# Moving one VectorE subtraction ahead in the turnover between two sub-layers

## The chip, the cores and the metric

The program runs on one core of a Trainium2 chip: TensorE (PE; its weight loads are shown as PEld), VectorE (DVE), ScalarE (ACT), GpSimd (POOL) and SyncE (SP), which issues the weight transfers. The engines run their own instruction streams in order and meet only at semaphores. The metric is the device time of one execution in microseconds; lower is better.

## The reference, cut to what matters

Two groups of tokens, 128 context tokens and 256 latent ones (384 columns together), go through two layers. A layer is SwiGLU, token mixing, SwiGLU, so there are six sub-layers. Each is wrapped in the same way:

```
def pre_norm(x, mod, j, g):
    return rmsnorm(x, g) * (1 + mod_chunk(mod, 3 * j + 1)) + mod_chunk(mod, 3 * j)

def post_residual(x, out, mod, j, g, w):
    return x + w * mod_chunk(mod, 3 * j + 2) * rmsnorm(out, g)

xs = post_residual(xs, swiglu(pre_norm(xs, mod_s, 0, ...), w_in, w_out), mod_s, 0, norm_post, 0.5)
```

All is fp32. The change sits where `post_residual` of one sub-layer meets `pre_norm` of the next.

## The kernel before, in words

Activations lie with the model dimension on the partitions: X is eight tiles (d = 0 to 7) of 128 x 384. The input h of a sub-layer is also eight tiles, and each is kept as two numbers whose sum is the fp32 value: a high part HH, rounded by ScalarE to the type that TensorE multiplies in, and a low part HL, the rest. Weights are split likewise into WH and WL. A product is three matmuls: WH with HH, WH with HL, WL with HH.

Weights stream through a ring of six 1 MB slots (RAW); SyncE loads them, ScalarE makes WH (L395), VectorE or GpSimd makes WL (L409), and four halves of each lie ready for TensorE.

The stretch between two sub-layers is the turnover (L1157 and following on VectorE). There are five of them, for s = 1 to 5; the opening of the first sub-layer has code of its own. When the statistics of the old sub-layer's output are known, VectorE does for each tile d:

- `scale_y` (L1150): multiply the old output tile by its norm factor
- `add_y` (L1154): add it to X, which gives the new X tile
- `scaled` (L1103): multiply X by the new norm factor, into TT; this signals h_scaled
- `full` (L1110, two instructions, one for each token group): h in full precision, into TT; only for tiles 0 and 1. For tiles 2 to 7 ScalarE does it (L724)
- `low` (L1117): HL = h - HH; this signals h_ready. It waits for the full h and for the high part

ScalarE makes the high part HH (L718, two instructions a tile) as soon as `scaled` of that tile is done, and signals h_hi. The VectorE order is written out by hand in the loop over d: `low` of tile d-1 comes behind `scaled` of tile d.

TensorE starts the next sub-layer with `pe_four` (L453 to L473), which takes four output columns at once and goes tile by tile through h. For tile 0 it waits for h_hi and does the eight products with HH (L453, L454), then waits for h_ready and does the four with HL (L457). Then comes `mod_pair` (L1556), small matmuls for the adaLN parameters, and then tile 1 to tile 7, twelve matmuls each (L462 to L464; the last tile L471 to L473), each tile behind its h_ready. Where the old sub-layer is a SwiGLU, `mod_pair` has 48 matmuls left there; where it is a mixer (turnovers two and five), 24.

Of the kernel before, what the change touches and what calls it, by code (L numbers as in the profile page):

```python
# [83 lines left out]
def summed_before(s):  # L84

    return sum(summed_slots(r) for r in range(s))
# [93 lines left out]
def trunk(nc, x_prompt, x_sample, c, state_hgrn, cache_k, cache_v, c_ctx, mod_w, mod_b, norm_pre, norm_post,  # L180
# [5 lines left out]
    with ctx:  # L186
# [213 lines left out]
        def split_dve(e, st, jj, nk, i=0):  # L400

            out = []
            p, _ = ring_at(st, jj)
            m = stages[st]["m"] + jj
            for b in range(2):
                def half(b=b):
                    k = (2 * m + b) % 4
                    e.wait_ge(half_hi, i * 12 + (2 * m + b + 1))
                    e.tensor_tensor(WL[:, k, 0:nk, :], RAW[:, p, 0:nk, b * P:(b + 1) * P],  # L409
                                    WH[:, k, 0:nk, :].bitcast(F32), ALU.subtract).then_inc(half_ready, 1)  # L410
                out.append(half)
            return out
# [64 lines left out]
        def cols3(t):  # L477
            return t[:, 0:NT]

        def rows_of(n):  # L480

            b, t = divmod(n, TOKS)
            return XS[:, t, b * 512:(b + 1) * 512]

        def sum_out(B, k):

            return B[:, 0:6 * SUM_COLS].rearrange("p (t k n) -> p t k n", t=TOKS, k=2)[:, :, k, 0]
# [539 lines left out]
        def _(dve):  # L1027
# [67 lines left out]
            def one_over(at, n):  # L1095
                dve.wait_ge(root_done, n)
                dve.reciprocal(STAT[:, at + 1, :], STAT[:, at, :]).then_inc(rstd_done, 1)

            def scaled(s, d):
                if d >= 2:  # L1100
                    dve.wait_ge(h_hi, 8 * s + d - 1)
                    dve.wait_ge(h_full, 8 * s + d - 1)
                dve.tensor_tensor(TT[:, d % 2, :], X[:, d, :], cols3(bank[5]), ALU.mult).then_inc(h_scaled, 1)  # L1103

            def full(s, d):
                dve.wait_ge(h_scaled, 8 * s + d + 1)
                if d >= 2:
                    dve.wait_ge(h_ready, 8 * s + d - 1)
                for g, (t0, t1) in enumerate(GROUPS):
                    x = dve.tensor_scalar(TT[:, 2 + d % 2, t0:t1], TT[:, d % 2, t0:t1], CA[:, s, d, g:g + 1],  # L1110
                                          MOD[:, 24 * s + d, g:g + 1], ALU.mult, ALU.add)
                x.then_inc(h_full, 1)

            def low(s, d):
                dve.wait_ge(h_full, 8 * s + d + 1)
                dve.wait_ge(h_hi, 8 * s + d + 1)
                dve.tensor_tensor(HL[:, d, :], TT[:, 2 + d % 2, :], HH[:, d, :].bitcast(F32),  # L1117
                                  ALU.subtract).then_inc(h_ready, 1)

            def add_terms(s, d, OUT):  # L1120

                if d == 0 and s == 5:
                    return
                if d == 0:
                    if s in SUMMED:
                        dve.wait_ge(mod_reduced, summed_before(s) + SUMMED_IN)
                    dve.wait_ge(out_done, 4 + 8 * s + 1)
                    dve.tensor_tensor(ROOT[:], X[:, 0, :], OUT[:, 0, :], ALU.mult).then_inc(xy_done, 1)
                    dve.wait_ge(coef_ready, 3 * s + 3)
                    last = CC[:, s, 7, :].rearrange("p (g n) -> p g n", n=1).broadcast_to([P, 2, SUM_COLS])  # L1130
                    dve.tensor_tensor(W7[:, :, 1, :], last, last, ALU.mult)
                    return
                dve.wait_ge(out_sq, 8 * s + d + 1)
                dve.wait_ge(sq_added, 6 * s + d - 1)
                dve.tensor_tensor(ACC[:], ACC[:], SQ[:, d % 2, :], ALU.add).then_inc(sq_added, 1)
                if s == 5:
                    return
                dve.wait_ge(out_sqy, 7 * s + d + 1)
                dve.wait_ge(y_added, 6 * s + d - 1)
                dve.tensor_tensor(RSTD[:], RSTD[:], TT[:, 2 + d % 2, :], ALU.add).then_inc(y_added, 1)  # L1140
                dve.wait_ge(out_done, 4 + 8 * s + d + 1)
                dve.wait_ge(xy_added, 6 * s + d - 1)
                dve.tensor_tensor(TT[:, 0, :], X[:, d, :], OUT[:, d, :], ALU.mult).then_inc(xy_done, 1)
                dve.wait_ge(xy_done, 8 * s + d + 1)
                dve.tensor_tensor(ROOT[:], ROOT[:], TT[:, 0, :], ALU.add).then_inc(xy_added, 1)

            def scale_y(s, OUT, d):
                dve.wait_ge(row_bcast, 2 * s + 2)
                dve.wait_ge(out_done, 4 + 8 * s + d + 1)
                dve.tensor_tensor(OUT[:, d, :], OUT[:, d, :], cols3(bank[4]), ALU.mult).then_inc(y_scaled, 1)  # L1150

            def add_y(OUT, d, n):
                dve.wait_ge(y_scaled, n)
                dve.tensor_tensor(X[:, d, :], X[:, d, :], OUT[:, d, :], ALU.add).then_inc(x_new, 1)  # L1154

            def turnover(s, OUT, n):

                add_terms(s, 6, OUT)
                if s < 5:
                    split_dve(dve, f"in{s + 1}", 1, 8)[0]()  # L1160
                if s < 5:
                    dve.wait_ge(out_sq, 8 * s + 8)
                    dve.tensor_tensor(TT[:, 1, :], X[:, 7, :], cols3(bank[7]), ALU.mult).then_inc(xy_done, 1)
                one_over(0, 2 * s + 2)
                if s == 5:
                    dve.wait_ge(rstd_done, 2 * s + 2)
                    for at in range(2 * TOKS):
                        dve.wait_ge(x_copied, at + 1)
                        dve.wait_ge(out_rows, at + 1)
                        dve.scalar_tensor_tensor(rows_of(at), bank[4 + at % 3][:], STAT[:, 1, at % TOKS:at % TOKS + 1],  # L1170
                                                 rows_of(at), ALU.mult, ALU.add).then_inc(y_ready, 1)
                    return
                sum_y2, sum_xy = sum_out(bank[0], 1), sum_out(bank[1], 0)
                r, a, q = STAT[:, 1, :], STAT[:, 2, :], STAT[:, 3, :]
                dve.wait_ge(rstd_done, 2 * s + 2)
                dve.wait_ge(stat_done, 2 * s + 2)
                dve.tensor_tensor(a, sum_y2, r, ALU.mult).then_inc(sum_step, 1)
                dve.wait_ge(sum_step, 5 * s + 1)
                dve.scalar_tensor_tensor(a, sum_xy, 2.0, a, ALU.mult, ALU.add).then_inc(sum_step, 1)
                dve.wait_ge(sum_step, 5 * s + 2)  # L1180
                dve.tensor_tensor(q, a, r, ALU.mult).then_inc(sum_step, 1)
                dve.wait_ge(sum_step, 5 * s + 3)
                dve.tensor_tensor(q, q, STAT[:, 4, :], ALU.add).then_inc(sum_step, 1)
                dve.wait_ge(sum_step, 5 * s + 4)
                dve.tensor_scalar(STAT[:, 4, :], q, 0.0, None, ALU.max).then_inc(sum_step, 1)
                scale_y(s, OUT, 0)
                one_over(5, 2 * s + 3)
                add_y(OUT, 0, 8 * s + 1)
                s += 1
                if s - 1 in SUMMED:  # L1190
                    dve.wait_ge(mod_reduced, summed_before(s))
                dve.wait_ge(row_bcast, 2 * s + 1)
                dve.wait_ge(x_new, 8 * (s - 1) + 1)
                scaled(s, 0)
                dve.wait_ge(coef_ready, 3 * s + 2)
                full(s, 0)
                for d in range(1, KD):
                    scale_y(s - 1, OUT, d)
                    add_y(OUT, d, 8 * (s - 1) + d + 1)
                    dve.wait_ge(x_new, 8 * (s - 1) + d + 1)  # L1200
                    scaled(s, d)
                    low(s, d - 1)
                    if d == 1:
                        full(s, d)
                low(s, KD - 1)
                dve.wait_ge(half_ready, 2 * stages[f"in{s}"]["m"] + 4)

            def ffn(s):
# [29 lines left out]
                for n in range(11):  # L1238
# [7 lines left out]
                    if n % 3 == 2:  # L1246
                        for b in range(2):
                            add_terms(s, 2 * (n // 3) + b, OUTF)
                turnover(s, OUTF, 11)

            def even(s):
# [778 lines left out]
```

## Time and profile before

| | us |
|---|---|
| median of 3 runs | 1619.7 (1615.0 to 1620.96) |
| the profiled execution | 1618.15 |
| its span in the trace | 1616.0 |
| PE busy | 1557.0 (96%) |
| DVE busy | 1094.1 (68%) |
| ACT busy | 688.3 (43%) |
| POOL busy | 42.1 (3%) |

TensorE is busy nearly all the time; the mean granted TensorE clock is 0.993 of full. The transfers keep the DMA engines about half busy on average (48.5% for the weights' queue).

### The profile page before, as it was taken

What the parts mean: (1) busy time and instruction counts of PE and PEld (TensorE: products, weight loads), DVE (VectorE), ACT (ScalarE), POOL (GpSimd) and SP (SyncE); (2) the same over time, 40 slices, a digit from 0 to 9 for tenths busy, and PEclk for the clock granted to TensorE, in tenths of its full rate; (3) what the DMA queues carried; (4) which work ended last, traced back from release to release, by engine and by line L of the source; (5) the groups of instructions that cost most, each with busy time, mean ns of one, the idle gap of its engine ahead of it and who ended that gap; (6) DMA issues with size and microseconds to landing.
All of it is one profiled execution on the core that took longest, in us unless ns stands there. A gap on an engine that the chain in (4) does not pass through costs nothing.

```text
span 1616.0 us, 25015 instructions
## 1 busy us (share of the span) xinstructions
PE 1557.0 (96%) x10103; PEld 1522.9 (94%) x10103; DVE 1094.1 (68%) x1991; ACT 688.3 (43%) x1198; POOL 42.1 (3%) x46
## 2 busy tenths in 40 slices
PE   5999999999989989999999999999999999999999
PEld 4999999999778989999999999999999989999998
DVE  5678889764659887788865787886462875443332
ACT  4433334464654466333344633334453266333333
POOL 2000000002100000000000000000000000000000
PEclk8999999999999999999999999999999999999999
DMA  9765656567220245656554565565463344443321
GB/s 327 250 209 169 199 174 218 192 210 228 70 91 27 92 149 166 208 174 198 178 176 136 184 202 188 183 195 170 131 209 124 112 153 160 131 130 114 107 66 39
DMA packets 255681, 260.07 MB, mean 161 GB/s; under 512 B 6625, under 2 KB 253826, under 8 KB 255570
## 3 DMA queue, kind: packets, MB, share of 16 engines
q1 hardware_dynamic: 250528, 253.25, 48.5%
q0 software_dynamic: 928, 2.44, 0.6%
q10 hardware_dynamic: 4114, 2.84, 0.6%
q8 instruction: 78, 1.28, 0.3%
q14 instruction: 33, 0.27, 0.1%
HBM read 255.88 MB, written 2.62 MB: 160 GB/s over the span
## 4 chain that ended last, share of the span: by engine, by line
PE 82%; DVE 10%; ACT 4%; issue 3%; POOL 1%; DMA 1%; ACTq 0%; DVEq 0%; POOLq 0%
PE bank L440 24%; PE bank L441 24%; PE bank L442 24%; DVE PARTS L1088 1%; DVE WL L409 1%; ACT WH L395 1%; PE bank L462 1%; PE bank L1614 1%; PE bank L463 1%; PE bank L464 1%; DVE X L1154 1%; PE bank L1911 1%; DVE HL L1117 1%; DVE SUMS L1419 1%; POOL WL L409 1%
## 5 line engine op out<-in xcount | busy, mean ns | idle before, releaser
L409 DVE TENSOR_TENSOR WL<-RAW,WH 128x1024 fp32r<-128x1024 f32 (+1 forms) x335 | 398.2, 1193 | 419.0 <-ACT WH L395 418.0
L395 ACT ACTIVATE WH<-RAW 128x1024 fp32r<-128x1024 f32 (+1 forms) x344 | 357.5, 1043 | 605.5 <-PE bank L442 593.4
L440 PE MATMUL bank<-HH,WH 128*128 128x384 f32 x1664 | 564.1, 339 | 8.0 <-DVE WL L409 3.5
L442 PE MATMUL bank<-HH,WL 128*128 128x384 f32 x1664 | 560.3, 337 | 0.0
L441 PE MATMUL bank<-HL,WH 128*128 128x384 f32 x1664 | 560.2, 337 | 0.0
L440 PEld LDWEIGHTS bank<-HH,WH 128*128 128x128 f32 x1664 | 313.9, 189 | 9.8 <-issue 3.9
L441 PEld LDWEIGHTS bank<-HL,WH 128*128 128x128 f32 x1664 | 313.7, 189 | 0.0
L442 PEld LDWEIGHTS bank<-HH,WL 128*128 128x128 f32 x1664 | 313.5, 188 | 0.0
L440 PE MATMUL bank<-AH,WH 128*128 128x384 f32 x704 | 237.0, 337 | 0.0
L441 PE MATMUL bank<-AL,WH 128*128 128x384 f32 x704 | 236.6, 336 | 0.0
L442 PE MATMUL bank<-AH,WL 128*128 128x384 f32 x704 | 236.6, 336 | 0.0
L1088 DVE SCALAR_TENSOR_TENSOR SUMS<-RAW,COND,SUMS 128x256 f32<-128x256 f32 x420 | 176.1, 478 | 0.0
L440 PEld LDWEIGHTS bank<-AH,WH 128*128 128x128 f32 x704 | 132.3, 188 | 0.1
L441 PEld LDWEIGHTS bank<-AL,WH 128*128 128x128 f32 x704 | 132.4, 188 | 0.0
L442 PEld LDWEIGHTS bank<-AH,WL 128*128 128x128 f32 x704 | 132.4, 188 | 0.0
L805 ACT ACTIVATE AH<-TT 128x384 fp32r<-128x384 f32 x88 | 45.7, 519 | 108.8 <-DVE TT L1226 108.8
L462 PE MATMUL bank<-HH,WH 128*128 128x384 f32 x192 | 66.6, 347 | 4.5 <-DVE HL L1117 2.9
L464 PE MATMUL bank<-HH,WL 128*128 128x384 f32 x192 | 64.7, 337 | 0.0
L463 PE MATMUL bank<-HL,WH 128*128 128x384 f32 x192 | 64.7, 337 | 0.0
L718 ACT ACTIVATE HH<-TT,MOD,CA 128x128 fp32r<-128x128 f32 x96 | 47.3, 540 | 33.2 <-DVE TT L1103 31.7
L1088 DVE SCALAR_TENSOR_TENSOR PARTS<-RAW,COND,PARTS 128x256 f32<-128x256 f32 x140 | 56.3, 477 | 0.0
L1231 DVE TENSOR_TENSOR AL<-TT,AH 128x384 fp32r<-128x384 f32 x88 | 48.8, 554 | 5.5
(244 smaller groups left out, 1470.3 us busy)
## 6 DMA issues: line engine op xcount, KB each, us to landing
RAW<-in_ffn_w_in SPq DMA_DIRECT2D x88, 1024.0 KB, 5.2
RAW<-in_mod_w SPq DMA_DIRECT2D x72, 1024.0 KB, 5.0
RAW<-in_ffn_w_out SPq DMA_DIRECT2D x32, 1024.0 KB, 5.2
RAW<-in_ab_w_in SPq DMA_DIRECT2D x16, 1024.0 KB, 5.9
RAW<-in_ffn_w_out SPq DMA_DIRECT2D x16, 768.0 KB, 4.4
RAW<-in_cv_w_in SPq DMA_DIRECT2D x12, 1024.0 KB, 5.2
RAW<-in_ab_w_out SPq DMA_DIRECT2D x4, 1024.0 KB, 5.2
RAW<-in_cv_w_out SPq DMA_DIRECT2D x4, 1024.0 KB, 5.2
```

The source lines that it names most:

```text
L395: e.activation(WH[:, (2 * m + b) % 4, 0:nk, :], RAW[:, p, 0:nk, b * P:(b + 1) * P], ACT.Copy).then_inc(half_hi, 1)
L409: e.tensor_tensor(WL[:, k, 0:nk, :], RAW[:, p, 0:nk, b * P:(b + 1) * P], WH[:, k, 0:nk, :].bitcast(F32), ALU.subtract).then_inc(half_ready, 1)
L440: e.matmul(out, WH[:, k, kk, :], xh(kk), start=(first and kk == 0), stop=False)
L441: e.matmul(out, WH[:, k, kk, :], xl(kk), start=False, stop=False)
L442: mm = e.matmul(out, WL[:, k, kk, :], xh(kk), start=False, stop=(last and kk == nk - 1))
L462: e.matmul(outs[b], WH[:, kh[b], kk, :], HH[:, kk, :], start=False, stop=False)
L463: e.matmul(outs[b], WH[:, kh[b], kk, :], HL[:, kk, :], start=False, stop=False)
L464: e.matmul(outs[b], WL[:, kh[b], kk, :], HH[:, kk, :], start=False, stop=False)
L718: a = act.activation(HH[:, d, t0:t1], TT[:, d % 2, t0:t1], ACT.Identity, bias=MOD[:, 24 * s + d, g:g + 1], scale=CA[:, s, d, g:g + 1])
L805: act.activation(AH[:, bass.ds(i * 6 + (j + b), 1), :], TT[:, 2 + b:3 + b, :], ACT.Copy).then_inc(act_hi, 1)
L1088: x = dve.scalar_tensor_tensor(a[:, g, :], w, by, a[:, g, :], ALU.mult, ALU.add)
L1231: dve.tensor_tensor(AL[:, at, :], TT[:, 2 + b:3 + b, :], AH[:, at, :].bitcast(F32), ALU.subtract).then_inc(act_ready, 1)
```

## The change

In the turnover VectorE now makes the low part of tile 0 directly behind `full` of tile 0, ahead of `scale_y`, `add_y` and `scaled` of tile 1. The loop makes the low part of tile d-1 only for d over 1. The opening of the first sub-layer is untouched, and so are all instructions of the other engines.

```
                 full(s, 0)
+                low(s, 0)
                 for d in range(1, KD):
                     scale_y(s - 1, OUT, d)
                     add_y(OUT, d, 8 * (s - 1) + d + 1)
                     dve.wait_ge(x_new, 8 * (s - 1) + d + 1)
                     scaled(s, d)
-                    low(s, d - 1)
+                    if d > 1:
+                        low(s, d - 1)
                     if d == 1:
                         full(s, d)
                 low(s, KD - 1)
```

VectorE in the turnover into the second sub-layer, from `scaled` of tile 0 to `scaled` of tile 2 (L1103 scaled, L1110 full, L1150 scale_y, L1154 add_y, L1117 low), before:

```order
270 L1103 TENSOR_TENSOR TT<-X,bank 128x384 [waits x_new,row_bcast,mod_reduced]
271 L1110 TENSOR_SCALAR TT<-TT,CA,MOD 128x128 [waits h_scaled,coef_ready]
272 L1110 TENSOR_SCALAR TT<-TT,CA,MOD 128x256
273 L1150 TENSOR_TENSOR OUTF<-OUTF,bank 128x384 [waits out_done,row_bcast]
274 L1154 TENSOR_TENSOR X<-X,OUTF 128x384 [waits y_scaled]
275 L1103 TENSOR_TENSOR TT<-X,bank 128x384 [waits x_new]
276 L1117 TENSOR_TENSOR HL<-TT,HH 128x384 [waits h_hi,h_full]
277 L1110 TENSOR_SCALAR TT<-TT,CA,MOD 128x128 [waits h_scaled]
278 L1110 TENSOR_SCALAR TT<-TT,CA,MOD 128x256
279 L1150 TENSOR_TENSOR OUTF<-OUTF,bank 128x384 [waits out_done,row_bcast]
280 L1154 TENSOR_TENSOR X<-X,OUTF 128x384 [waits y_scaled]
281 L1103 TENSOR_TENSOR TT<-X,bank 128x384 [waits h_full,h_hi,x_new]
```

The same place on VectorE after the change:

```order
270 L1103 TENSOR_TENSOR TT<-X,bank 128x384 [waits x_new,row_bcast,mod_reduced]
271 L1110 TENSOR_SCALAR TT<-TT,CA,MOD 128x128 [waits h_scaled,coef_ready]
272 L1110 TENSOR_SCALAR TT<-TT,CA,MOD 128x256
273 L1117 TENSOR_TENSOR HL<-TT,HH 128x384 [waits h_hi,h_full]
274 L1150 TENSOR_TENSOR OUTF<-OUTF,bank 128x384 [waits out_done,row_bcast]
275 L1154 TENSOR_TENSOR X<-X,OUTF 128x384 [waits y_scaled]
276 L1103 TENSOR_TENSOR TT<-X,bank 128x384 [waits x_new]
277 L1110 TENSOR_SCALAR TT<-TT,CA,MOD 128x128 [waits h_scaled]
278 L1110 TENSOR_SCALAR TT<-TT,CA,MOD 128x256
279 L1150 TENSOR_TENSOR OUTF<-OUTF,bank 128x384 [waits out_done,row_bcast]
280 L1154 TENSOR_TENSOR X<-X,OUTF 128x384 [waits y_scaled]
281 L1103 TENSOR_TENSOR TT<-X,bank 128x384 [waits h_full,h_hi,x_new]
```

The subtraction for tile 0, with its wait for ScalarE's high part, has moved up past three instructions; what stood between `scaled` and `full` of tile 1 is gone, and the number of instructions is the same.

## Rows read from the trace of the kernel before

**Rows 1.** Page, section 1: busy time of each engine.

```profile
PE 1557.0 (96%) x10103; PEld 1522.9 (94%) x10103; DVE 1094.1 (68%) x1991; ACT 688.3 (43%) x1198; POOL 42.1 (3%) x46
```

**Rows 2.** Source L1117 (low): who waited for it (us, times).

```profile
  PEld bank L462: 5.0, 8
  PEld bank L457: 1.7, 5
```

**Rows 3.** Timeline, VectorE, first turnover: start, length, line, tiles [idle before].

```profile
322.15 0.56 DVE L1103 TENSOR_TENSOR TT<-X,bank 128x384 f32<-128x384 f32 x1 [0.58 <-PE bank L1621]
322.81 0.67 DVE L1110 TENSOR_SCALAR TT<-TT,CA,MOD 128x128 f32<-128x128 f32 x2
323.40 0.55 DVE L1150 TENSOR_TENSOR OUTF<-OUTF,bank 128x384 f32<-128x384 f32 x1
323.98 0.56 DVE L1154 TENSOR_TENSOR X<-X,OUTF 128x384 f32<-128x384 f32 x1
324.57 0.55 DVE L1103 TENSOR_TENSOR TT<-X,bank 128x384 f32<-128x384 f32 x1
325.04 0.55 DVE L1117 TENSOR_TENSOR HL<-TT,HH 128x384 fp32r<-128x384 f32 x1
325.51 0.66 DVE L1110 TENSOR_SCALAR TT<-TT,CA,MOD 128x128 f32<-128x128 f32 x2
326.09 0.54 DVE L1150 TENSOR_TENSOR OUTF<-OUTF,bank 128x384 f32<-128x384 f32 x1
...
327.26 0.55 DVE L1103 TENSOR_TENSOR TT<-X,bank 128x384 f32<-128x384 f32 x1
327.73 0.55 DVE L1117 TENSOR_TENSOR HL<-TT,HH 128x384 fp32r<-128x384 f32 x1
...
329.85 0.55 DVE L1117 TENSOR_TENSOR HL<-TT,HH 128x384 fp32r<-128x384 f32 x1
```

**Rows 4.** Timeline, ScalarE, same turnover: high parts of tiles 0 and 1.

```profile
322.80 0.98 ACT L718 ACTIVATE HH<-TT,MOD,CA 128x128 fp32r<-128x128 f32 x2 [1.96 <-DVE TT L1103]
...
325.16 0.99 ACT L718 ACTIVATE HH<-TT,MOD,CA 128x128 fp32r<-128x128 f32 x2 [1.38 <-DVE TT L1103]
```

**Rows 5.** Timeline, end of the turnover: ScalarE's full tile 7, VectorE's low 7.

```profile
339.31 0.98 ACT L724 ACTIVATE TT<-TT,MOD,CA 128x128 f32<-128x128 f32 x2
340.32 0.56 DVE L1117 TENSOR_TENSOR HL<-TT,HH 128x384 fp32r<-128x384 f32 x1 [1.47 <-ACT TT L724]
```

**Rows 6.** Timeline, TensorE and its weight loads, same turnover.

```profile
325.65 0.65 PEld L457 LDWEIGHTS bank<-HL,WH 128*128 128x128 f32 x4 [0.46 <-DVE HL L1117]
...
326.55 1.52 PE L1556 MATMUL bank<-RAW,COND 128*32 128x128 f32 x48
...
328.34 0.19 PEld L462 LDWEIGHTS bank<-HH,WH 128*128 128x128 f32 x1 [0.55 <-DVE HL L1117]
...
336.79 0.19 PEld L462 LDWEIGHTS bank<-HH,WH 128*128 128x128 f32 x1
```

**Rows 7.** Timeline, TensorE, second turnover: the first matmul of tile 1.

```profile
604.66 0.45 PE L462 MATMUL bank<-HH,WH 128*128 128x384 f32 x1 [0.93 <-DVE HL L1117]
```

**Rows 8.** Chain that ended last, behind the first turnover: start, us, what.

```profile
341.88 1.07 ACT WH L395
343.05 1.23 DVE WL L409
```

**Rows 9.** Timeline, VectorE: `full` of tiles 0 and 1, second and fifth turnover.

```profile
599.13 0.67 DVE L1110 TENSOR_SCALAR TT<-TT,CA,MOD 128x128 f32<-128x128 f32 x2
601.83 0.66 DVE L1110 TENSOR_SCALAR TT<-TT,CA,MOD 128x128 f32<-128x128 f32 x2
...
1325.79 0.67 DVE L1110 TENSOR_SCALAR TT<-TT,CA,MOD 128x128 f32<-128x128 f32 x2
1328.49 0.66 DVE L1110 TENSOR_SCALAR TT<-TT,CA,MOD 128x128 f32<-128x128 f32 x2
```

**Rows 10.** Windows, TensorE: length, busy (instructions), granted clock, DMA share, GB/s.

```profile
504.00:510.00 6.00, 4.34 (x36) 1.00 0.00 0
508.00:514.00 6.00, 5.02 (x25) 0.72 0.25 79
599.00:605.00 6.00, 4.76 (x79) 1.00 1.09 359
```

More of the change, by code:

```diff
@@ L1196, in turnover @@
                 full(s, 0)
+                low(s, 0)
                 for d in range(1, KD):
@@ L1201, in turnover @@
                     scaled(s, d)
-                    low(s, d - 1)
+                    if d > 1:
+                        low(s, d - 1)
                     if d == 1:
```

## The prediction, made before the changed kernel ran

> **What bounds the kernel now.** Read the busy shares first: TensorE works 1557.0 of 1616.0 us [rows 1], so a change pays or costs only where TensorE waits, and every microsecond that is added to such a wait goes to the end unless something later gives it back. Then ask who waits for the instruction that moves, `low`: TensorE's weight loads wait for it 5.0 us in 8 cases ahead of a later tile (L462) and 1.7 us in 5 cases ahead of the products with HL of tile 0 (L457) [rows 2]. The 1.7 us, about 0.3 us in each turnover, are what an earlier low part of tile 0 can take away. The question is what the move does to the 5.0 us.
>
> The timeline of the first turnover answers it. TensorE stands 0.46 us for low 0, runs its four products and 48 small matmuls (1.52 us from 326.55, so done by 328.07), and then its loader stands for low 1, which ends at 328.28 (327.73 + 0.55); it starts at 328.34 [rows 3, 6]. From there VectorE delivers a low part every 2.12 us (327.73, 329.85) [rows 3], and TensorE takes a tile in (336.79 - 328.34) / 4 = 2.11 us [rows 6]. So TensorE follows VectorE tile by tile with no slack: a low 1 that comes x later ends the sub-layer's first four columns x later. Low 0 bounds nothing; behind it TensorE waits for low 1 anyway.
>
> **What the change does to VectorE.** No instruction is added. Three things move.
>
> First, the wait. Behind `full` 0 VectorE now goes on at once with `scale_y` 1, at 323.40 [rows 3]. In its place stands low 0, which needs the high part of tile 0. ScalarE starts that at 322.80 and takes 0.98 us, so it ends at 323.78 [rows 4]. How long VectorE needs from there: for low 7 the releaser ends at 339.31 + 0.98 = 340.29 and low 7 starts at 340.32, 0.03 us later [rows 5]. So low 0 starts at about 323.82, and VectorE stands idle 0.42 us that it did not stand before. In the old order the wait was free, since `scale_y`, `add_y` and `scaled` of tile 1 covered it.
>
> Second, low 0 itself: a slot of 0.47 us (325.04 to 325.51) leaves its old place and costs 0.47 us in the new one. Net nothing.
>
> Third, what it hid in its old place. `full` 1 reads what `scaled` 1 wrote and waits for its completion. Now low 0 lies between them: `scaled` 1 at 324.57, low 0 at 325.04, `full` 1 at 325.51. Without it `full` 1 stands directly behind `scaled` 1, as `full` 0 stands behind `scaled` 0: 322.15 to 322.81, 0.66 us from start to start [rows 3], where an instruction that waits for nothing follows after 0.47 us. That is 0.66 - 0.47 = 0.19 us more.
>
> Worked through: low 0 at 323.82, `scale_y` 1 at 324.29, `add_y` 1 at 324.87 (0.58 behind), `scaled` 1 at 325.46 (0.59 behind), `full` 1 at 326.12, `scale_y` 2 at 326.70 (0.58 behind, as before). It was at 326.09, so 0.61 us later, and everything behind keeps its distances: `scaled` 2 at 327.87, low 1 at 328.34 instead of 327.73. The high part of tile 1 starts some 0.59 us behind `scaled` 1 (325.16 behind 324.57) and takes 0.99 us [rows 4]; that makes 327.04, in time for low 1. The ScalarE chain of tiles 2 to 7 starts from `scaled`, and it moves by the same 0.61.
>
> At this point the Trainium skill has a rule against my third term. The row shows 0.66 us from start to start with a semaphore between the two and 0.47 us without one that holds [rows 3]. The page "VectorE: DVE Perf Modes", section "The DRAIN you can't avoid", says that the next instruction waits for the pipeline to empty in any case and that "the semaphore costs nothing extra here". By that rule the third term is zero and the change costs 0.42 us a turnover; by the row it costs 0.61. The trace does not agree with the rule, and I go by the row.
>
> **On TensorE.** The 0.46 us wait at L457 goes, in all turnovers 1.7 us together [rows 2]. The small matmuls then run that much earlier, and the wait for low 1 is longer by the same amount plus 0.61 us: in the first turnover 0.55 + 0.46 + 0.61 = 1.6 us, in the second, with half as many small matmuls, 0.93 us [rows 7] grows to about 1.7. No other work of TensorE lies there to fill it. Behind the four columns the next weights follow in a chain that starts from TensorE itself: ScalarE's WH at 341.88, VectorE's WL at 343.05 [rows 8]. It shifts too and gives nothing back. No transfer is issued from VectorE, and SyncE's ring is served on average at half load, so a slot that comes free 0.6 us later is no bound.
>
> **The sum.** All five turnovers have the same VectorE rhythm: `full` 0 to `full` 1 takes 2.70 us in the first (322.81 to 325.51) [rows 3], in the second (599.13 to 601.83) and in the fifth (1325.79 to 1328.49) [rows 9]. So 5 x 0.61 = 3.05 us. Made against the profiled execution's own time: 1618.15 + 3.05 = 1621.2 us, which is +0.19%. The median of the runs shown is 1619.7, 1.6 us above that execution; on it the same sum would stand at 1622.75, and the range leans up for that.
>
> The unknown is the new wait. At least 0.38 us (323.78 - 323.40) and no gap behind `scaled` 1: 1.9 us in all. At most a release as slow as that of WL by WH, 343.05 against 341.88 + 1.07 = 342.95, 0.10 us [rows 8]: 0.48 + 0.19 = 0.67, or 3.35 us. A gain is excluded as long as the high part ends behind `full` 0. I take 0.61, since low 7 is the same instruction with the same kind of releaser.
>
> **The rivals.**
>
> *The delay is the wait alone.* By the rule above `full` 1 starts 0.47 us behind `scaled` 1: 5 x 0.42 = 2.1 us, 1620.25 us. Against it: `full` 0 behind `scaled` 0.
>
> *It is swallowed.* If VectorE could catch up within the eight tiles, or a later wait took it in, the time stays at 1618.15. For it: TensorE has 59 us of idle in other places [rows 1]. Against it: the two paces, 2.12 and 2.11 us, leave nothing to catch up with.
>
> *Faster.* The wait at L457 goes and low 1 comes no later: 1618.15 - 1.7 = 1616.45 us. This decides only if the high part of tile 0 is through by 323.40, when VectorE gets there; ScalarE needs 0.98 us and starts in the same moment as VectorE's `full`, which takes 0.67 [rows 3, 4]. The profile speaks against it by 0.38 us. Even then low 1 must be earlier for TensorE to gain.
>
> *Slower by more: the TensorE clock.* In the window 504 to 510 us TensorE is busy 4.34 of 6 us at full clock, and the window 508 to 514 behind it has a granted clock of 0.72, a stretch at 1.2 instead of 2.4 GHz, which costs (1 - 0.72) x 6 = 1.7 us of work [rows 10]. In the second turnover TensorE is now busy 4.76 of 6 us at clock 1.00 [rows 10]; with the change it would be about 4.2, below 4.34. If the clock falls in the two turnovers behind mixers, 3.05 + 2 x 1.7 = 6.4 us, 1624.6 us; if in all five, 3.05 + 8.4 = 11.5, 1629.6 us. Against it: the waits of before, up to 0.93 us [rows 7], left the clock at 1.00, and the other three turnovers keep twice as many small matmuls in the gap. The page "TensorE: Matmul & The Clock Gate", section "The HAM clock gate", holds the same: idleness brings the slow level, activity releases it; the trace agrees, with 0.72 behind a thin stretch.
>
> **Chances.** Forecast 1621.2: 0.65. The wait alone, 1620.25: 0.12. Swallowed: 0.08. Faster, 1616.45: 0.05. Clock in two turnovers: 0.06; in all five: 0.04. The order shows the instruction moved in every turnover, so that the change does nothing is not a case apart. The runs of before spread from 1615.0 to 1620.96, about 3 us around their middle, and that is wider than my unknowns; a measurement can tell 0.5%, some 8 us, from no change. The range that should hold 8 in 10 is 1617 to 1625.5. Faster by over 0.5% needs under 1611.6: 0.02. Slower by over 0.5% needs over 1627.8, only the clock in all turnovers or something unseen: 0.05. The same: 0.93.
>
> **What would show it.** Right: VectorE idle of about 0.4 us ahead of L1117 in five places with ScalarE's HH (L718) as releaser; `full` 0 to `full` 1 3.3 instead of 2.70 us, `scaled` 1 to `full` 1 0.66; the weight loads' wait at L457 gone and that for L462 up from 0.55 to about 1.6 us; each turnover's first tile-1 matmul 0.6 us later against `scaled` 0. Wrong: an idle of zero ahead of low 0, an unchanged distance from `scaled` 0 to low 1, or a granted clock below 1.00 in the turnovers.

## The result and the profile after

The changed kernel is slower: 1624.14 us in the median of 10 runs (1620.74 to 1626.83) beside 1618.38 us before; the ratio is 1.0032 with a 95% interval of 1.0019 to 1.0045, some 5.2 us. In a second series it was 1.0043 (1.0030 to 1.0056). The ten runs fall into two groups that go with TensorE's mean granted clock: five took 1620.7 to 1623.1 us at 0.992 or 0.993, five took 1625.2 to 1626.8 us at 0.989 to 0.991. The profiled execution took 1622.41 us, its span is 1620.2 us, 4.2 above the span of before.

The same VectorE rows as in [rows 3], of the kernel after (start, length, line, tiles; in brackets the idle time before):

```profile
322.07 0.55 DVE L1103 TENSOR_TENSOR TT<-X,bank 128x384 f32<-128x384 f32 x1 [0.58 <-PE bank L1623]
322.73 0.67 DVE L1110 TENSOR_SCALAR TT<-TT,CA,MOD 128x128 f32<-128x128 f32 x2
323.81 0.56 DVE L1117 TENSOR_TENSOR HL<-TT,HH 128x384 fp32r<-128x384 f32 x1 [0.41 <-ACT HH L718]
324.28 0.55 DVE L1150 TENSOR_TENSOR OUTF<-OUTF,bank 128x384 f32<-128x384 f32 x1
...
325.46 0.55 DVE L1103 TENSOR_TENSOR TT<-X,bank 128x384 f32<-128x384 f32 x1
326.05 0.67 DVE L1110 TENSOR_SCALAR TT<-TT,CA,MOD 128x128 f32<-128x128 f32 x2
...
328.28 0.55 DVE L1117 TENSOR_TENSOR HL<-TT,HH 128x384 fp32r<-128x384 f32 x1
```

VectorE stands idle 0.41 us ahead of low 0, for ScalarE's high part. `full` 1 starts 0.59 us behind `scaled` 1. From `full` 0 to `full` 1 it is 3.32 us (2.70 before), from `scaled` 0 to low 1 it is 6.21 us (5.58 before): 0.63 us.

TensorE's side. The first row is of the weight loads in the first turnover, to be held against [rows 6]; the second is of the matmuls in the second turnover, to be held against [rows 7]. At this place the loads show 0.27 us more idle time than the matmuls, so the two rows are not to be compared with one another: on the matmuls' rows the wait ahead of tile 1 is 1.80 us behind the two mixers and 1.1 to 1.3 us in the other three turnovers.

```profile
328.88 0.19 PEld L462 LDWEIGHTS bank<-HH,WH 128*128 128x128 f32 x1 [1.58 <-DVE HL L1117]
...
604.16 0.44 PE L462 MATMUL bank<-HH,WH 128*128 128x384 f32 x1 [1.80 <-DVE HL L1117]
```

The waits around `low` in all turnovers, to be held against [rows 2]. The first line is VectorE's new wait for ScalarE; the second shows that the weight loads' wait ahead of later tiles has almost doubled, from 5.0 us. Their wait at L457 is gone.

```profile
  ACT HH L718: 2.0, 5
...
  PEld bank L462: 9.7, 8
```

Something else is in the trace of after. These are windows of TensorE (length, busy, granted clock, DMA share, GB/s) around the fifth turnover, behind the convolution mixer:

```profile
1328.00:1334.00 6.00, 4.20 (x76) 1.00 1.07 354
1334.00:1340.00 6.00, 5.74 (x24) 0.72 1.09 348
```

Behind the stretch of 4.20 busy microseconds in six, tile 1 begins at 1334.26 us, and for 3.4 us the granted clock is 1.2 instead of 2.4 GHz. The matmuls there stand 0.32 us apart instead of 0.17.

A second such fall lies in the convolution mixer (the odd token mixer, between the fourth and the fifth turnover), which the change does not touch. TensorE pauses there for 3.0 us ahead of the output projection, before the change and after it; the pause ends at 1282.72 us before and at 1283.49 after. These are the windows behind it, first before, then after:

```profile
1282.00:1288.00 6.00, 5.28 (x30) 1.00 0.56 178
...
1283.00:1289.00 6.00, 5.51 (x23) 0.72 0.56 178
```

### The profile page after: what moved, and what is told of

Its sections match the earlier page's. It is cut to its first block, busy times and chain, and to the rows that moved or that the text cites. A ratio compares the mean times of both kernels' runs of the same rounds, so it can differ in the third digit from the quotient of the medians.

```text
span 1620.2 us, 25015 instructions
## 1 busy us (share of the span) xinstructions
PE 1557.5 (96%) x10103; PEld 1526.1 (94%) x10103; DVE 1095.1 (68%) x1991; ACT 688.3 (42%) x1198; POOL 42.1 (3%) x46
## 4 chain that ended last, share of the span: by engine, by line
PE 82%; DVE 10%; ACT 3%; issue 3%; POOL 1%; DMA 0%; ACTq 0%; DVEq 0%; POOLq 0%
PE bank L440 24%; PE bank L441 24%; PE bank L442 24%; PE bank L462 1%; DVE WL L409 1%; DVE PARTS L1088 1%; PE bank L463 1%; PE bank L464 1%; ACT WH L395 1%; PE bank L1616 1%; DVE X L1154 1%; DVE SUMS L1421 1%; POOL WL L409 1%; DVE MIX L1385 1%; PE bank L1913 1%
```

## Where the time went, by stretches

The beginning of `full` 0 in each of the five turnovers (T1 to T5) cuts the trace into pieces, each of which holds one turnover. The table gives how much longer each piece is than in the profile of before (287.76, 287.77, 151.13 and 290.17 us); "t" marks a piece with a clock fall at the tile 1 behind the turnover, "c" one in the convolution mixer, ahead of its output projection. The first piece, T1 to T2, is left out: with the even token mixer in it, it varies from 273.8 to 278.0 us over the profiles (276.3 before), in both directions. Each row is one profile, while the ratio is of all runs of that kernel, so the two need not add up.

| kernel | T2 to T3 | T3 to T4 | T4 to T5 | T5 to end | ratio |
|---|---|---|---|---|---|
| changed, 1st profile | 0.64 | 0.63 | 2.18 c | 1.94 t | 1.0032 |
| changed, 2nd profile | 1.96 t | 0.61 | 3.26 c | 0.62 | 1.0043 |
| wait_only | 0.45 | 0.44 | 2.00 c | 0.43 | 1.0026 |
| low0_behind_scale | 0.05 | 0.05 | 0.05 | 0.05 | 1.0001 |
| after_cover | 0.41 | 0.40 | 1.96 c | 0.41 | 1.0018 |
| after_fill | 1.22 | 0.95 | 0.88 | 1.18 | 1.0041 |
| after_fill_small | 0.64 | 0.60 | 2.20 c | 1.80 | 1.0037 |
| full1_act | -0.57 | -0.24 | 1.06 c | -0.58 | 0.9989 |
| interleaved | -1.35 | -0.48 | -0.93 | -2.10 | 0.9971 |
| after_swiglu_only | 0.01 | 0.63 | 2.20 c | 0.01 | 1.0022 |
| after_mixers_only | 1.96 t | -0.01 | 1.59 c | 1.93 t | 1.0038 |
| after_fill_both | 0.66 | 0.64 | 0.62 | 0.63 | 1.0020 |

The undisturbed pieces of the changed kernel show VectorE's delay alone, 0.63 us; each "t" adds 1.3 us, each "c" 1.6 us (2.6 in the second profile, where the slow stretch was twice as long). One number has another source: of the 1.80 in after_fill_small, 1.2 us lie behind the last instruction of every compute engine (4.0 us from VectorE's last to the end of the span, 2.8 in all other profiles), so the end of a run adds noise of that size too.

## The experiments

**The wait by itself.** wait_only:

```
                 full(s, 0)
+                dve.wait_ge(h_hi, 8 * s + 1)
                 for d in range(1, KD):
```

> The order of before; VectorE only waits, behind full 0 and ahead of scale_y 1, for ScalarE's high part of tile 0. Low 0 stays where it was, behind scaled 1. This buys the wait by itself. Theory (wait 0.42 us and uncovered full 1 0.19 us a turnover, both passed on to TensorE): full 0 to full 1 goes from 2.70 to 3.12 us, the time up by 5 x 0.42 = 2.1 us, some 1.0013 of before. Rival, the cost of the change is the wait alone: the same 3.12 here, but then the changed kernel's 3.3 us must be found elsewhere. Rival, a falling TensorE clock makes up the rest of the measured 5 us: here the wait at L457 grows as well, so the stretch is as thin, and the time is up 4 to 5 us with a mean granted clock of 0.989 to 0.992 in some runs.

Measured 1.0026 (1.0016 to 1.0036). `scale_y` 1 waits 0.33 us for ScalarE; `full` 0 to `full` 1 is 3.12 us as forecast, and the clean pieces are 0.44 us longer:

```profile
323.69 0.55 DVE L1150 TENSOR_TENSOR OUTF<-OUTF,bank 128x384 f32<-128x384 f32 x1 [0.33 <-ACT HH L718]
```

So most of the 0.63 us is the wait. The total is 4.2 us instead of 2.1. In the profile 1.6 us of it are the fall in the convolution mixer, so the clock rival had a part in it, though in another place than it named: no turnover shows a fall.

**The move without the wait.** low0_behind_scale puts low 0 one instruction later than the changed kernel does:

```
-                low(s, 0)
                 for d in range(1, KD):
                     scale_y(s - 1, OUT, d)
+                    if d == 1:
+                        low(s, 0)
                     add_y(OUT, d, 8 * (s - 1) + d + 1)
```

> Low 0 one instruction further back than in the changed kernel: behind scale_y 1, where ScalarE's high part (ready at about 1.0 us behind the start of full 0) is through. Theory: no idle time ahead of low 0; the gap scaled 1 to full 1 is 0.66 us, and low 0 now fills the 0.11 us that add_y waited for scale_y; full 0 to full 1 = 2.70 + 0.19 - 0.11 = 2.78 us; the time up by 5 x 0.08 = 0.4 us, not to be told from before (0.999 to 1.001). The TensorE wait at L457 is gone here too, so whoever holds that low 0 bounds the start expects 1.7 us less than before. Rival, the clock: the gap ahead of tile 1 is still wider than before, so the time would stay 1 to 2 us up.

Measured 1.0001 (0.9992 to 1.0009); `scaled` 1 to `full` 1 is 0.59 us, `full` 0 to `full` 1 is 2.73 us (2.78 forecast), and the pieces are +0.05. Low 0 is early here as well, TensorE no longer waits for it, and nothing is gained: low 0 bounds nothing.

**The uncovered `full` 1.** after_cover moves `scale_y` 2 ahead of `full` 1:

```
                 for d in range(1, KD):
-                    scale_y(s - 1, OUT, d)
+                    if d != 2:
+                        scale_y(s - 1, OUT, d)
...
                     if d == 1:
+                        scale_y(s - 1, OUT, 2)
                         full(s, d)
```

> The changed kernel, with scale_y 2 moved up between scaled 1 and full 1, so that full 1 waits for nothing uncovered. Theory: the wait of 0.42 us ahead of low 0 stays; scaled 1 to full 1 is 0.94 us of which 0.47 is scale_y 2 itself; scale_y 2 to add_y 2 is covered too; low 1 comes 0.3 us earlier than in the changed kernel and 0.3 us later than before: 5 x 0.31 = 1.5 us above before, 1.001. Rival, that a semaphore between neighbours costs nothing: low 1 as late as in the changed kernel, time as there, 1.0032. Rival, the clock: 3 to 4 us above before, with a mean clock under 0.993.

Measured 1.0018 (1.0009 to 1.0027); the wait ahead of low 0 is again 0.41 us, and the clean pieces are +0.40 instead of +0.63. The cover returns 0.23 us a turnover (forecast 0.3): neighbours that depend on one another do cost. In total it is 2.9 us against a forecast of 1.5; the profile has 1.6 us of that in the convolution mixer's fall, with none in the turnovers.

**Idle matmuls against the clock, first size.** after_fill puts 8 or 12 of them behind the small matmuls:

```
+                    for _ in range(8 if SUBLAYERS[s - 1][0] == "ffn" else 12):
+                        pe.matmul(bank[7][:, 384:512], ONES[:], IDENT[:], start=True, stop=True)
```

> The changed kernel, with idle matmuls (128 x 128, ones by identity, into columns of a bank that nobody reads) on TensorE between the small matmuls and tile 1: 8 of them behind a SwiGLU, 12 behind a mixer, some 1.0 and 1.5 us by 0.12 us each, which fit into the wait for low 1. VectorE is as in the changed kernel, and the results are the same. Theory: TensorE waits anyway, so the time is the changed kernel's by VectorE's delay, before + 3 us, and if the clock never mattered it is also what the changed kernel has, 1.0032. Rival, the clock: the stretch is as busy as before, the granted clock falls no more often than before, mean 0.992 to 0.993 in all runs, and the time is 1.5 to 2.5 us under the changed kernel's, 1.0018 to 1.002. If a filler runs past low 1 the time rises instead.

Neither the theory nor the rival came, but the case of the last sentence: 1.0041 (1.0028 to 1.0053). Each turned out to be two matmuls in the trace, 2.05 and 2.94 us in all, and they ran past low 1. Tile 1 begins 7.22 us behind `scaled` 0 in the first turnover and 7.65 in the second, instead of 6.82, so the turnovers are later by 0.4 to 0.8 us than in the changed kernel.

**The changed kernel again, and fewer idle matmuls.** The second has 4 and 6 in place of 8 and 12.

> The changed kernel once more, beside the other kernels of this call, for its ratio and its granted clock on the same chip. Theory, VectorE's 0.61 us a turnover and nothing else: 3.1 us above before, 1.0019, clock as before (mean 0.994). Rival, that and a clock that falls more often because TensorE waits longer ahead of tile 1: 4.5 to 5.5 us above before, 1.003, mean clock 0.991 to 0.992.

> The kernel with idle matmuls on TensorE behind the small matmuls of tile 0, now 4 behind a SwiGLU and 6 behind a mixer, by the measured 0.245 us each 1.0 and 1.5 us, which end ahead of low 1 (8 and 12 of them took 2.05 and 2.94 us and ran past it). VectorE and the results as in the changed kernel. Rival, the clock: TensorE is as busy there as before the change, the mean clock goes back to 0.993 to 0.994, and the time is 3 us above before, 1.0018 to 1.002, 1.5 to 2.5 us under the changed kernel of the same call. If the clock falls for other reasons (the 3.0 us pause in the convolution mixer, the scans of the even mixer), the clock and the time are the changed kernel's.

The changed kernel gave 1.0043 (1.0030 to 1.0056) with a mean clock of 0.991 over its runs (before: 0.994), 7 us, on the rival's side. (A fall of 3.4 us to half the clock lowers the mean over 1620 us by 0.001, so this is some three falls an execution more than before.) Its profile has the clock fall at tile 1 of the second turnover. With 4 and 6 idle matmuls no fall is left in the turnovers, but the fall in the convolution mixer is still there, and the ratio is 1.0037 (1.0025 to 1.0050), with a mean clock of 0.992, where 1.0018 to 1.0020 was forecast: filling the turnovers alone did not bring the time down.

**By place.** early_low is true in after_swiglu_only where the old sub-layer is a SwiGLU, in after_mixers_only where it is a mixer:

```
-                low(s, 0)
+                early_low = SUBLAYERS[s - 1][0] == "ffn"
+                if early_low:
+                    low(s, 0)
...
-                    if d > 1:
+                    if d > 1 or not early_low:
                         low(s, d - 1)
```

> Low 0 ahead of scale_y 1 only in the three turnovers whose old sub-layer is a SwiGLU (1, 3, 4); the two behind the mixers as before. There the TensorE wait ahead of tile 1 grows only to some 1.6 us with twice as many small matmuls beside it, and no profile showed the clock fall there. Theory (VectorE's 0.61 us everywhere, clock falls only behind the mixers): 3 x 0.61 = 1.8 us above before, 1.0011, apart from what the convolution mixer's own pause costs by chance. Rival, that the cost above 3 us has nothing to do with the mixers' turnovers: three fifths of 1.0037, so 1.0022.

> The reverse: low 0 ahead only in the two turnovers behind the mixers (2, 5). Theory: 2 x 0.61 = 1.2 us, and in a part of the executions 1.3 us more for each turnover in which the granted clock falls at tile 1 (the wait there grows from 0.93 to 1.8 us): 1.2 to 3.8, some 1.0015, with a mean clock below before's. Rival, unrelated to the place: two fifths of 1.0037, 1.0015 as well, but with the clock of before; the window of six us from tile 1 on tells them apart, 0.72 or 1.00 in the profile.

Three turnovers: 1.0022 (1.0013 to 1.0031). Two turnovers: 1.0038 (1.0025 to 1.0051), more than twice what five turnovers would share out to two, above both forecasts of 1.0015, and with the lower clock (0.991) that the first of them named. The first is 3.6 us, twice its forecast and just what its rival, three fifths of the whole, had named; but that rival needs 1.0015 for the two turnovers and falls with them. Its profile has the 1.9 us of VectorE and the 1.6 us fall in the convolution mixer, and none in a turnover. The profile of the second has the fall in both places. TensorE there (matmuls, then windows):

```profile
604.27 0.86 PE L1560 MATMUL bank<-RAW,COND 128*32 128x128 f32 x24
606.92 0.45 PE L462 MATMUL bank<-HH,WH 128*128 128x384 f32 x1 [1.79 <-DVE HL L1117]
...
607.39 0.52 PE L464 MATMUL bank<-HH,WL 128*128 128x384 f32 x1
```

```profile
606.00:612.00 6.00, 5.08 (x20) 0.72 1.10 347
...
1336.00:1342.00 6.00, 4.88 (x19) 0.72 1.09 349
```

Twenty-four small matmuls, 1.79 us of nothing, then matmuls of 0.52 us, where one takes 0.34 us at full clock.

**Both kinds of gap filled.** after_fill_both has the 4 and 6 idle matmuls and ten more in the convolution mixer's pause:

```
-                for _ in out_four(s, range(KD), lambda kk: pe.wait_ge(cat_ready, 8 + kk + 1)):
+                steps = out_four(s, range(KD), lambda kk: pe.wait_ge(cat_ready, 8 + kk + 1))
+                for _ in range(10):
+                    pe.matmul(bank[7][:, 384:512], ONES[:], IDENT[:], start=True, stop=True)
+                for _ in steps:
                     pass
```

> The changed kernel with the small idle matmuls of before in the turnovers (4 and 6) and ten more, 2.4 us, in TensorE's 3.0 us pause ahead of the convolution mixer's output projection. Results the same. If the clock's falls in those two kinds of place are what the changed kernel costs above VectorE's 3 us, none is left in them: 3 us above before, less the 0 to 1.6 us that before itself loses in that pause in some executions, 1.001 to 1.002. If not, it stays at 1.0037.

Measured 1.0020 (1.0011 to 1.0029), 3.2 us, with the clock of before (0.994), although VectorE runs as in the changed kernel. The windows around the second and the fifth turnover, in that kernel:

```profile
604.00:610.00 6.00, 5.74 (x56) 1.00 1.10 351
...
1334.00:1340.00 6.00, 5.73 (x36) 1.00 1.08 354
```

All four pieces are 0.62 to 0.66 us above before. What is left is VectorE's part, five times 0.63. The kernel of before was not run with idle matmuls, so how much of its own time they would save is not known.

**The other way: VectorE sooner at low 1.** full1_act lets ScalarE make `full` 1:

```
-                high_parts(s + 1, 2)
+                high_parts(s + 1, 1)
...
-                    if d == 1:
-                        full(s, d)
```

> The order of before; ScalarE makes full 1 as it makes full 2 to 7, VectorE's two instructions for it (0.58 us of slot) go. If low 1 is what TensorE waits for in every turnover, low 1 comes 0.58 us earlier: behind a mixer TensorE gains 0.58 us, behind a SwiGLU it gains only until its small matmuls end, some 0.3 us; 2 x 0.58 + 3 x 0.3 = 2.1 us under before, 0.9987. A rival that low 0 bounds the start, or that a later wait takes VectorE's time back, expects no change.

Measured 0.9989 (0.9981 to 0.9998), as forecast (0.9987), although its profile has the fall in the convolution mixer. The pieces with one turnover behind a mixer are 0.57 and 0.58 us shorter, the one behind a SwiGLU 0.24 (0.58 and 0.3 forecast): what counts is when low 1 is there.

interleaved has that and this loop, and `scale_y` 1 ahead of the wait for `scaled` 0:

```
+                scale_y(s - 1, OUT, 1)
...
-                full(s, 0)
                 for d in range(1, KD):
-                    scale_y(s - 1, OUT, d)
                     add_y(OUT, d, 8 * (s - 1) + d + 1)
+                    if d < KD - 1:
+                        scale_y(s - 1, OUT, d + 1)
+                    if d == 1:
+                        full(s, 0)
                     dve.wait_ge(x_new, 8 * (s - 1) + d + 1)
                     scaled(s, d)
                     low(s, d - 1)
-                    if d == 1:
-                        full(s, d)
```

> No VectorE instruction stands directly behind the one whose result it reads: scale_y of tile d+1 between add_y d and scaled d, low d-1 between scaled d and add_y d+1, scale_y 1 ahead of scaled 0 in VectorE's 0.58 us of idle, full 0 behind add_y 1 and scale_y 2; and full 1 on ScalarE as in the run before. A tile then takes 4 x 0.47 = 1.88 us on VectorE instead of 2.12, and TensorE's own 2.10 us a tile is the bound. Low 1 would end some 1.0 us earlier; the wait ahead of tile 1 goes behind a SwiGLU (gain 0.8 us) and nearly so behind a mixer (gain 1.0 us): 3 x 0.8 + 2 x 1.0 = 4.5 us under before, 0.9972. If gaps between neighbours cost nothing (the rule of the Trainium skill, VectorE: DVE Perf Modes, The DRAIN you can't avoid), only the part of full 1 on ScalarE is gained: 2.1 us.

Measured 0.9971 (0.9960 to 0.9981), 1613.63 us: as forecast (0.9972), and faster than both kernels. Its VectorE rows, from low 0 on:

```profile
324.57 0.55 DVE L1117 TENSOR_TENSOR HL<-TT,HH 128x384 fp32r<-128x384 f32 x1
325.04 0.55 DVE L1154 TENSOR_TENSOR X<-X,OUTF 128x384 f32<-128x384 f32 x1
325.50 0.55 DVE L1150 TENSOR_TENSOR OUTF<-OUTF,bank 128x384 f32<-128x384 f32 x1
325.97 0.55 DVE L1103 TENSOR_TENSOR TT<-X,bank 128x384 f32<-128x384 f32 x1
326.58 0.56 DVE L1117 TENSOR_TENSOR HL<-TT,HH 128x384 fp32r<-128x384 f32 x1
```

The starts are 0.47 us apart where 0.58 and 0.59 stood (low 1 comes 0.61 us behind `scaled` 2, since it waits for `full` 1 from ScalarE), and low 1 is 4.46 us behind `scaled` 0 (322.12 in this kernel) instead of 5.58.

> The interleaved turnover (0.9971) with the ten idle matmuls in the convolution mixer's pause. The clock's fall there cost 1.6 us in profiles that had it; in executions that had it, it goes: 0 to 1.6 us under the interleaved kernel, 0.9965 to 0.9971, and a narrower spread of the runs.

With the ten idle matmuls as well it was 0.9971 again (0.9958 to 0.9983), 1612.97 us: no gain that can be told, and the interleaved kernel's profile had no fall there to take away.

## Why the prediction was right, and where it was short

- **What bounds.** Right. TensorE waits for low 1; low 0 moved and its wait went, and nothing came of it (low0_behind_scale).
- **The wait ahead of low 0.** 0.42 us forecast. ScalarE's release took 0.10 us (high part done at 322.72 + 0.99 = 323.71, low 0 at 323.81), as WL's behind WH in [rows 8], and not 0.03: low 0 came 1.08 us behind `full` 0, where `scale_y` 1 had stood 0.59 us behind it, so the wait cost 0.49. In wait_only it was 0.44.
- **The uncovered `full` 1.** 0.19 us forecast from `full` 0 behind `scaled` 0 (0.66); the gap was 0.59 us from start to start, so 0.59 - 0.47 = 0.12. `full` 0 is no fair pattern for it: the order lists show that it has a second wait, for coef_ready, which `full` 1 has not. That this makes the 0.07 us is likely and was not tried. The two errors cancel, by luck: 0.61 forecast, 0.61 by these two, 0.63 in the pieces. after_cover took 0.23 back with two gaps covered. That such a neighbour costs nothing does not hold for these instructions.
- **TensorE has nothing to fill the gap, and passes the delay on.** Right: the wait for low 1 was forecast at 1.6 us for the weight loads of the first turnover and at 1.7 us for the matmuls of the second; they are 1.58 and 1.80 us, and the undisturbed pieces grew by 0.63 us, 5 x 0.63 = 3.15 us against 3.05.
- **The sum and the rivals.** Short. Of the measured 5.2 and 7.0 us the sum has 3.05. That 1624.14 lies in the range of 1617 to 1625.5 is owed to the width of the range and not to the sum. What the sum leaves out is the TensorE clock, which stood among the rivals with 0.06 for "the two turnovers behind mixers": 1618.15 + 3.05 + 3.4 = 1624.6 us. A granted clock below 1.00 in the turnovers is what the prediction itself had named as a sign of being wrong, and the profile has it in the fifth. That the rival's time comes near the measured 1624.14 is in part luck, for it knew nothing of the fall in the convolution mixer. Its mechanism was told rightly (a stretch thinner than the 4.34 of 6 us in [rows 10]), its chance was far too low: in the three profiles with a wait of 1.8 us behind the mixers, the clock fell in four of six such turnovers. In the 6 us up to tile 1 TensorE was busy 3.9 us there, not the forecast 4.2; in after_cover, with a wait of 1.5 us and 4.2 us busy, the clock fell in none of two. The price of a fall was told at 1.7 us and is 1.3 us, so two turnovers by four sixths by 1.3 = 1.8 us on average, an estimate from few profiles. 3.1 + 1.8 = 4.9 us, or 6.5 with the 1.6 us of the convolution mixer, beside the 5.2 and 7.0 measured. The chance should have gone by the busy time that the sum itself implied, less than in the stretch that had been seen to lose the clock.
- **Not foreseen at all:** the fall in the convolution mixer, where the change touches nothing. Only filling that pause as well as the turnovers (after_fill_both) brought the time to VectorE's part alone.

What stays open is that last one. TensorE pauses 3.0 us there in every kernel but the two that fill it, and is busy without a break in the 6 us before. In the profiles of before, low0_behind_scale, after_fill and interleaved the clock held; in the changed kernel's two, wait_only, after_cover, after_fill_small, full1_act and the two by place it fell. Where the profile has it, the ratio is higher by about as much (wait_only 4.2 us against 2.2 for VectorE's part, after_swiglu_only 3.6 against 1.9), so it seems to be tied to the kernel more than to chance. The mean clock over all runs points the same way: 0.994 for low0_behind_scale, as before, and 0.993 for wait_only, after_swiglu_only and full1_act, which is the size of one fall of 3.4 us. But full1_act is faster, and it fell there too. Whether an earlier or later arrival at the pause decides it was not tried.

## What to carry to other kernels

Before an instruction is moved ahead of others, ask what the move puts behind its wait: here 0.4 to 0.5 us of wait that three instructions had covered went straight onto the chain that TensorE follows, while the consumer of the moved instruction stood at its next wait anyway. On VectorE put an independent instruction between two that depend on one another. And when a change lengthens a wait of TensorE, look in the trace for a stretch in which TensorE was busy as little: if the clock fell behind that one, a fall belongs into the sum, with a chance, and not among the far rivals. It does not come each time: here the same stretch kept the clock in one profile of a kernel and lost it in the next. When the difference is as small as this, compare the pieces of the trace and not only the totals.

## What the hardware showed that was not expected

- A fall of the granted clock to 1.2 GHz for 3.4 us behind a wait of only 1.8 us, where the neighbouring matmuls were small ones, in four of six cases; it cost 1.3 us. In the three other turnovers, with waits of 1.1 to 1.3 us on the same rows and twice as many small matmuls beside them, there was none. Which of the two differences decides was not tried.
- The same 3.0 us pause lost the clock in some kernels and not in others, 1.6 us or, in one profile, 2.6 us.
- Two VectorE instructions of 0.55 us start 0.47 us apart when they are independent, and 0.58 or 0.59 us apart when the second reads what the first wrote (0.66 for `full` 0, which has a second wait).
